# Two-map attention: value products on split operands over pairs of query tiles, with the copies and differences of the turned weights placed behind the exponentials

## What is computed

```python
def diff_attention(q, k, v, pos, slopes, lam):
    # q, k: [B, L, H, 2, d]; v: [B, L, H, 2d];  H = 8, d = 64, L = 1040
    scale = A_HEAD_DIM ** -0.5
    def block(qb, pb):
        s = jnp.einsum('bqhmd,bkhmd->bhmqk', qb, k).astype(jnp.float32) * scale
        ...
        s = s - slopes[None, :, None, None, None] * dist
        p = jax.nn.softmax(s, axis=-1)
        w = p[:, :, 0] - lam * p[:, :, 1]
        return jnp.einsum('bhqk,bkhe->bqhe', w.astype(v.dtype), v)
    return sweep_queries(block, q, pos[None])
```

## Time and profile before

| | us |
|---|---|
| time, median of 3 runs (3290.07 to 3292.62) | 3291.96 |
| time of the profiled execution | 3290.69 |
| its span, first to last instruction | 3288.9 |
| PE busy in it | 3188.6 (97%) |
| DVE busy | 1707.1 (52%) |
| ACT busy | 1131.5 (34%) |
| POOL busy | 997.7 (30%) |
| mean granted TensorE clock | 0.985 |

### The profile page before, as it was taken

The page is one execution under the profiler, slowest core; times in us unless marked ns, Lnnn a source line. Parts: engine busy times, 40 slices in busy tenths (PEclk is TensorE's granted clock), DMA queues, the critical chain, the costliest instruction groups (busy, mean ns, idle before and its releaser), DMA issues.

```text
span 3288.9 us, 52109 instructions
## 1 busy us (share of the span) xinstructions
PE 3188.6 (97%) x20350; PEld 2839.4 (86%) x20350; DVE 1707.1 (52%) x2867; ACT 1131.5 (34%) x2189; POOL 997.7 (30%) x688
## 2 busy tenths in 40 slices
PE   8999999999999999999999999999999999799997
PEld 6677768788888888999899899999999999699997
DVE  5554556765554535666666632277677033522223
ACT  3433333333332214555555541166465111300002
POOL 3112224787773333222222132210000223022222
PEclk9999999999999999999999999999999999799998
DMA  4011112122225112000000012211111341478888
GB/s 160 26 33 33 33 65 103 64 77 78 77 82 207 52 45 98 20 20 20 20 21 26 14 43 79 74 43 48 38 45 50 129 156 51 181 257 315 307 315 291
DMA packets 94214, 312.01 MB, mean 95 GB/s; under 512 B 14690, under 2 KB 27810, under 8 KB 90832
## 3 DMA queue, kind: packets, MB, share of 16 engines
q1 hardware_dynamic: 68448, 248.16, 21.3%
q10 hardware_dynamic: 19424, 42.70, 3.4%
q0 software_dynamic: 6160, 18.63, 2.3%
HBM read 247.91 MB, written 56.22 MB: 92 GB/s over the span
## 4 chain that ended last, share of the span: by engine, by line
PE 54%; DVE 3%; DMA 1%; ACT 1%; issue 1%; POOL 0%; SPq 0%; ACTq 0%; POOLq 0%; DVEq 0%
PE PS L673 14%; PE PS L3162 7%; PE PS L3631 6%; PE PS L661 5%; PE PS L3226 4%; PE PS L3378 4%; PE PS L3193 3%; PE PS L3661 3%; PE PS L3412 3%; PE PS L3454 2%; DVE EB L2837 1%; PE PS L3227 0%; DMA fin<-h_rows 0%; PE PS L3175 0%; DMA h_rows<-y_row_b,pick_s_b 0%
## 5 line engine op out<-in xcount | busy, mean ns | idle before, releaser
L695 POOL CAST w_hi<-ring 128x1024 fp32r<-128x1024 f32 x130 | 138.1, 1062 | 1543.9 <-PE PS L673 401.4
L697 POOL TENSOR_TENSOR w_lo<-ring,w_hi 128x1024 fp32r<-128x1024 f32 x130 | 333.4, 2565 | 10.5
L2247 ACT ACTIVATE EA<-EA,small_sb 128x1040 f32<-128x1040 f32 x144 | 166.6, 1157 | 186.4 <-DVE small_sb L2690 186.3
L2690 DVE CUSTOM_DVE_ANT_0 EA<-PS,biasH,low_a 128x1024 f32<-128x1024 f32 x128 | 163.6, 1278 | 56.3 <-PE PS L3193 56.2
L3162 PE MATMUL PS<-u_hi,w_hi 128*128 128x348 f32 x504 | 173.5, 344 | 0.0
L3162 PE MATMUL PS<-u_lo,w_hi 128*128 128x348 f32 x504 | 162.1, 322 | 0.0
L3162 PE MATMUL PS<-u_hi,w_lo 128*128 128x348 f32 x504 | 161.8, 321 | 0.0
L1643 DVE TENSOR_TENSOR hid_lo<-hid,hid_hi 128x1024 fp32r<-128x1024 f32 x44 | 91.7, 2123 | 118.8 <-ACT hid_hi L1285 118.8
L1735 PE MATMUL PS<-u_hi,w_hi 128*128 128x512 f32 x352 | 146.8, 417 | 3.0 <-POOL w_lo L697 2.3
L1932 PE MATMUL PS<-t_hi,slot_hi 128*128 128x512 f32 x352 | 138.9, 395 | 5.9 <-DVE t_lo L1544 3.3
L3226 PE MATMUL PS<-Va,PTa 128*128 128x128 f32 (+1 forms) x1152 | 139.9, 275 | 0.0
(11 more groups left out here) (502 smaller groups left out, 8639.5 us busy)
## 6 DMA issues: line engine op xcount, KB each, us to landing
ring<-in_stream SPq DMA_DIRECT2D x130, 512.0 KB, 3.5
w_gate_sb<-in_w_gate SPq DMA_DIRECT2D x64, 512.0 KB, 6.8
w_up_sb<-in_w_up SPq DMA_DIRECT2D x64, 512.0 KB, 8.1
w_down_sb<-in_w_down SPq DMA_DIRECT2D x64, 512.0 KB
gu_raw<-in_gate_up SPq DMA_DIRECT2D x22, 1024.0 KB, 5.6
hid_keep<-hid_out SPq DMA_DIRECT2D x17, 512.0 KB, 2.9
hid<-hid_keep ACTq DMA_DIRECT2D x15, 512.0 KB, 16.4
x_keep<-xT ACTq DMA_DIRECT2D x1, 4176.0 KB, 13.8
```

Of the source, the lines that this page charges most:

```text
L695: pool.tensor_copy(w_hi[j][:, :, :], w_raw[j][:, :, :]).then_inc(S["w_rounded"], 1)
L697: pool.tensor_tensor(w_lo[j][:, :, :], w_raw[j][:, :, :], w_hi[j][:, :, :], ALU.subtract).then_inc(S["w_split"], 1)
L2247: act.activation(e[0:m, :], e[0:m, :], ACT.Exp, scale=-1.0, bias=small[0:m, 8 + 2 * par + k:9 + 2 * par + k], accum_out=small[0:m, 12 + 2 ...
L2690: dve.tensor_tensor_reduce(e[0:m, 0:T1], wide(2 * k, T1, m), bias, -1.0, low_a[0:m, t, k:k + 1], ALU.add, ALU.min, low).then_inc(S["aa_max ...
```

## The change

The value products of attention a are made of split parts over groups of tiles, (0,1), (2,3), (4,5) and (6,7,8). The weights' columns of a group (256, or 272 in the last) are now the moving operand and v the stationary one, so the result is turned: features by tokens. ACT copies it (`take_columns`), PE turns it back (`turn_back`), and ACT writes the scaled rows (`results`). The turned weights are copied by ACT in three instructions per tile (`take_pt`, 16 + 512 + 512 columns) and subtracted by DVE in three (`lower_probs`); v gets the same (`lower_values`). PA_hi and PA_lo exist once. The room for them is taken from o_tok: rows of tiles 5 to 8 are staged and stored to a DRAM tensor o_keep by ACT, 64 KB at a time, and read back in four transfers after the last head. The squares are behind the copies now, and the two exponentials have at most a `take_columns` between them.

```diff
+A_GROUPS = ((0, 1), (2, 3), (4, 5), (6, 7, 8))
+HELD = 5
...
 (ACT, head)
-                        if last:
-                            take_pt_meta(h, par, t, False)
                         if after:
                             exp(after[0], (after[1] + after[2]) % 2, after[2], 0)
-                        if before and not last:
-                            square(*before)
-                        if not last:
-                            take_pt_meta(h, par, t, first and t < 2)
+                        if t % 2 == 0 and before:
+                            take_columns(*before)
                         if after:
                             exp(after[0], (after[1] + after[2]) % 2, after[2], 1)
+                        take_pt(h, t)
+                        if t % 2 and before:
+                            squares(*before)
...
 (DVE)
+                def lower_probs(h, t):
+                    m = P if t < NT else META
+                    n, cols = 9 * h + t, probs_slot(t)
+                    dve.wait_ge(S["aa_pt"], 3 * n + 1)
+                    dve.tensor_tensor(PA_lo[0:META, NT, cols], bank(7, m, 3 * P, META), PA_hi[0:META, NT, cols], ALU.subtract).then_inc(S["probs_lo"], 1)
+                    for b in range(2):
+                        tiles = slice(4 * b, 4 * b + 4)
+                        dve.wait_ge(S["aa_pt"], 3 * n + 2 + b)
+                        dve.tensor_tensor(PA_lo[:, tiles, cols], bank(5 + b).rearrange("p (j n) -> p j n", n=P)[:, :, 0:m], PA_hi[:, tiles, cols], ALU.subtract).then_inc(S["probs_lo"], 1)
...
+                def attend(h, par, t, fresh=False, lower=None):
                     scores(h, par, t, 0, fresh)
                     scores(h, par, t, 1, fresh)
                     combine(h, par, t, fresh)
+                    if lower:
+                        lower_probs(*lower)
...
-                            attend(h, (odd + t + 1) % 2, t + 1, first)
+                            attend(h, (odd + t + 1) % 2, t + 1, first, (h, t))
...
 (PE, turn_probs)
+                    for b in range(2):
+                        if n:
+                            pe.wait_ge(S["probs_lo"], 3 * (n - 1) + 2 + b)
...
+                def values(h, g, half):
+                    n, w = 9 * h + A_GROUPS[g][-1], group_width(g)
+                    pe.wait_ge(S["probs_lo"], 3 * n + 2 + half)
+                    if g == 0:
+                        pe.wait_ge(S["values_lo"], 3 * h + 2 + half)
+                    for i in (range(4, NT + 1) if half else range(4)):
+                        v_hi, v_lo = (Va_hi[:, i, :], Va_lo[:, i, :]) if i < NT else (Vam_hi[:, :], Vam_lo[:, :])
+                        for k, (v, probs) in enumerate(((v_hi, PA_hi), (v_hi, PA_lo), (v_lo, PA_hi))):
+                            last = mm(bank(7, w), v, probs[:, i, 0:w], start=(i == 0 and k == 0), stop=(i == NT and k == 2))
...
+                def turn_back(h, g, n):
+                    pe.wait_ge(S["columns_in"], NGA * h + g + 1)
+                    pe.wait_ge(S["probs_lo"], 3 * n + 1)
...
 (PE, head: scores of t+1, then)
+                        if before:
+                            values(*before, 1)
                         kind, c = UNITS[t]
                         unit(h + 1, 1 - odd, kind, c, 0)
                         turn_probs(h, (odd + t) % 2, t, first)
                         unit(h + 1, 1 - odd, kind, c, 1)
-                        if t >= 1:
-                            values(h, odd, t - 1, 18 * h + 2 * t + 1)
+                        if t in (1, 3, 5, NT):
+                            values(h, min(t // 2, NGA - 1), 0)
+                        if before:
+                            turn_back(*before, 9 * h + t)
...
 (POOL, after the last head)
                 for t in range(NT + 1):
+                    if t == HELD:
+                        pool.wait_ge(S["keep_ld"], 32 + 16 * SPILLED)
                     heads_norm(pool, t).then_inc(S["as_np"], 1)
```

More of the change, by code:

```diff
@@ new lines, in take_columns, with home, results @@
+                def take_columns(h, g):
+                    w = group_width(g)
+                    act.wait_ge(S["aa_o"], NGA * h + g + 1)
+                    act.activation(turned_back[:, 0:w], bank(7, w), ACT.Copy).then_inc(S["columns_in"], 1)
+                def home(h, t, m):
+                    return o_tok[0:m, t, bass.ds(h * P, P)] if t < HELD else stage[t - HELD][0:m, :]
+                def results(h, g):
+                    act.wait_ge(S["aa_v"], TURNED_A * h + 4 + g)
+                    if g == NGA - 1 and h + 1 < HEADS:
+                        act.wait_ge(S["values_lo"], 3 * (h + 1) + 1)
+                    for k, t in enumerate(A_GROUPS[g]):
+                        m = P if t < NT else META
+                        if t == HELD:
+                            act.wait_ge(S["keep_st"], KEPT + 16 * SPILLED * h)
+                        seen(act)
+                        act.activation(home(h, t, m), bank(7, P, k * P, m), ACT.Copy, scale=small[0:m, 48 + t:49 + t]).then_inc(S["aa_y"], 1)
@@ L2347, in _ @@
                 sigmoid(0, 0, EARLY_GATES[0], 0)
-                result(HEADS - 1, NT)
-                square(HEADS - 1, NT)
+                results(HEADS - 1, NGA - 1)
+                squares(HEADS - 1, NGA - 1)
                 roots(slice(HEADS - 1, HEADS))
+                act.wait_ge(S["keep_st"], KEPT + 16 * SPILLED * HEADS)
+                for t in range(HELD, NT + 1):
+                    m = P if t < NT else META
+                    act.dma_start(o_tok[0:m, t, :], o_keep[0:m, t - HELD, :]).then_inc(S["keep_ld"], 16)
                 for t in range(NT + 1):
@@ L3229, in head @@
+                def turn_back(h, g, n):
+                    pe.wait_ge(S["columns_in"], NGA * h + g + 1)
+                    pe.wait_ge(S["probs_lo"], 3 * n + 1)
+                    for k, t in enumerate(A_GROUPS[g]):
+                        m = P if t < NT else META
+                        last = turn(bank(7, P, k * P, m), turned_back[:, k * P:k * P + m])
+                    last.then_inc(S["aa_v"], 1)
                 def head(h, odd, first=False):
@@ L3235, in head @@
                             scores(h + 1, 1 - odd, 0)
-                        if t == 0:
-                            pe.wait_ge(S["aa_vf"], 3 * h + 3)
-                            if not first:
-                                pe.wait_ge(S["aa_pt"], 18 * h)
-                            turn(bank(6, P, 0, META), vTa[:, T1:T2]).then_inc(S["aa_v"], 1)
+                        before = None if first and t == 0 or t == NT or t % 2 else group_before(h, t)
+                        if before:
+                            values(*before, 1)
                         kind, c = UNITS[t]
```

260 lines of the change are left out of this document (142 added, 118 removed).

## The result

The changed kernel takes 3452.46 us (median of 4 runs, 3445.59 to 3452.87), the kernel before 3292.29 us (4 runs on the same chip). The ratio is 1.0482, 95% interval 1.0464 to 1.0500: slower by 160 us, where 118 were forecast. That lies inside the wide range (3350 to 3462), near its upper end, outside the forecast's own 3390 to 3435, and on the second rival's 3453.

The account below looks back on a forecast made before the run. PE's list bounds attention a before; afterwards waits between PE and DVE decide. Seven heads 60, last head 19, tail 7 and clock 32 make +118 us: 3410 us, own range 3390 to 3435, wide range 3350 to 3462.

Parts of the forecast that it names:

- the second rival: Clock falls behind nearly every wait, or POOL's 8.6 us stay, or low clock lengthens even steps: about 3453 us, chance 0.20.
- The odd ring: Attention a, odd t: PE's half value product waits for DVE's differences, made behind the next tile's combination; 9.9 us.
- The clock: Half speed behind PE's idle times: 14 in seven heads, five in the last, 19 x 1.7 = 32 us.
- POOL: What POOL's interference costs DVE per head of attention a: bounds 0 and 8.6 us, 4.3 taken.
- t = 0: First step of a head: the turned values wait for both halves of the differences, 9.7 us.
- Even steps: Attention a, even t: PE's list from scores to scores, 8.5 us, is longer than DVE's 8.3.
- The last head: Between reciprocals of tiles 1 and 8: +19 us from the same waits, plus 5 x 1.7 for low clock.
- the tail: After the last head: POOL's four norms and split wait for o_tok's loads; PE +7 us late, bounds +4 and +13.
- The first, that the clock holds: Rival: idle times leave the granted clock alone, so only 60 + 19 + 7 are added: 3378 us, chance 0.20.
- The halves are not waited for: Rival: differences are ready when PE comes to the first half, PE's shorter list makes it faster: 3262 us, chance 0.05.
- Only DVE's own list binds: Rival: DVE's waits for PE are hidden, its list makes 80.2 us a head: 3312 us, chance 0.07.
- PE's list: PE's work per head of attention a: 18.9 us removed, 13.1 and 1.2 added, shrinking by 4.6 us.

Follow-up runs that it names:

- Run 7: Changed kernel, with ACT's copies for odd t and t = 8 between the next exponentials and DVE's differences ahead of the reciprocals; PE's list untouched: 3312.49 us, ratio 1.0064.
- run 3: Changed kernel plus unread filler products in PE's waits ahead of the first halves of the value products, pricing the clock alone: 3405.89 us, ratio 1.0353.
- the last run of experiment 8: Changed kernel with halves, meta scores, copies, differences and tail work reordered, finally turn_back of three groups behind the next scores: 3284.04 us, ratio 0.9976.
- runs 4 and 5: Changed kernel, tail reordered: POOL's split ahead of its norms (3452.76 us); separately, DVE's lower parts of turned tiles 0 to 2 ahead of its norms (3450.51 us).
- run 2: Changed kernel with PE's first halves of value products and the meta scores moved behind the next step's scores: 3350.23 us, ratio 1.0177.
- run 6: Changed kernel with halves and meta scores behind the next scores, plus ACT's take_columns behind the second exponential: 3342.97 us, ratio 1.0159.

## Why the prediction was right, and where it was short

- **The odd ring.** Right. Passes, 1.40 for the exponential (1.53 where `take_columns` stands between), combination, differences, half product and scores follow as written, and PE's wait at t = 1 and 5 was 1.9 us for 2.0. Run 7 changed only the place of the copies and differences, and 140 of the 160 us went with it.
- **The clock: the term that was mis-sized.** The price was about right: 1.7 us each was worked out, t = 1 ran 1.8 and t = 5 1.7 over its ring, and run 3 has 1.5 and 1.6. The count was not. "Of four per head in seven heads I take 14" rested on idle times of 1.8 to 2.7 us. In the changed kernel seven waits were 5.0 us and seven were 3.1 to 3.8, and the clock fell behind all of them; of the fourteen near 1.9 us it fell behind eleven. With the last head's three that is 28 of 31. At t = 8 the fall costs 3.2 us in five heads, since the meta scores and the scores are at half speed too, and 1.5 in the two where the clock rose earlier. Over seven heads t = 1, 3 and 5 ran 31 us over their rings and t = 8, without POOL's part, 19: 50 us, where 24 were in the sum. That is 26 of the missing 42.
- **POOL.** "I take 4.3" between 0 and 8.6. The head shown has 1.6 at t = 2, 1.3 at t = 6, 1.9 at t = 7 and 0.85 at t = 8, 5.7 us, so 10 us more in seven heads. I had not followed the copy at t = 2 on: it also made t = 3's wait long enough for the clock to fall each time.
- **t = 0**, 10.5 for 9.7, makes up 5 us more over seven heads, and most of that is low clock again. Behind filled waits (run 3) it took 9.9 us in five of the heads. In the first head it took 11.6 us, where the clock fell behind a wait of 1.84 us ahead of `turn_values`, and 10.2 in the last run of experiment 8, where it held there. These three come to 41 of the 42 us.
- **Even steps.** Right: t = 4 took 8.6 us for 8.5, with PE idle next to nothing; t = 2 and 6 are this and POOL.
- **The last head**, +26.4 for +27.5, and **the tail**, +6.8 for +7, came out. In the last head four falls took the place of the five in the sum, behind its three halves and one `turn_back`. The tail came out by another path than the one written, runs 4 and 5: the term had POOL's norms and split in it, and DVE's lower parts behind the same loads ended later. That its size agreed was luck.
- **The rivals.** The second, the clock falling behind nearly every wait, had a chance of 0.20 and is what happened. Its 3453 us is close partly by luck, as it priced POOL higher than it was and t = 8 lower. The first, that the clock holds, is out with the same count. "The halves are not waited for" is out with the waits of 1.7 to 5.0 us. "Only DVE's own list binds" gave 80.2 us for a head. Run 7 has 80.1, but there the differences of odd t and t = 8 lie in a wait that the 80.2 count beside them, so the agreement shows nothing.
- **PE's list** was to shrink by 4.6 us a head, and shrank by 3.8. The value products of 256 columns stand 0.118 us apart (thirteen from 1618.43 to 1619.97), as the row of attention b said. The rest is spread over the list, as distances between starts over a head of the last run and of the kernel before show: the old value products took 18.7 us for the 18.9 taken, the new ones 13.3 for 13.1 and the turns back 0.9 for 1.2, while the half units take 0.4 us more than before and scores and meta scores 0.2. The Trainium skill (TensorE: Matmul & The Clock Gate, "Wait — 56ns, not 53.3ns?") has 0.109 there; here, where every product has a weight load of its own, the measured distance is 9% longer. Its rule for the low clock, N/1.2 GHz, gives 0.227 for 272 columns, and there the trace agrees (0.226).

## What to carry to other kernels

When an operand is made of parts, the part that is made last decides, and its place in its engine's list matters more than how long it takes: here the same three differences cost 140 us more behind a combination than ahead of it, in a wait that was there anyway. Price each wait of PE twice, once for itself and once for the half speed behind it, and follow a late start on another engine into the next wait before counting how many of them are long. And when an experiment takes a wait away, look one step on: in run 2 it stood there again, and the engine named by the longest idle time (run 6) was not its cause.

## What the runs showed of the hardware that I had not expected

- In the changed kernel's seven heads the granted clock fell behind 11 of the 14 idle times of 1.7 to 2.2 us ahead of the halves at t = 1 and 5, and held behind three of the same length (1.74, 1.78 and 1.89 us). Windows behind two idle times of 1.89 us, both at t = 5, one with a fall and one without:

```profile
1754.33:1759.33 5.00, 5.00 (x28) 4.83 (x30) 1.19 (x3) 0.00 (x0) 0.00 (x0) 0.66 0.02 3
1853.52:1858.52 5.00, 5.00 (x40) 4.43 (x41) 1.85 (x5) 0.00 (x0) 0.00 (x0) 1.00 0.00 0
```

Behind the seven waits of 1.4 to 1.5 us in run 7 it never fell. In run 7's last head, waits of 2.14 to 2.17 us before `turn_back` were followed by 0.80, 1.00 and 0.60 over 2 us. So the length of an idle time near 2 us does not decide alone; what else does, no run here shows.

- A copy of 16 columns on DVE (0.17 us) took 2.15 us beside POOL's split, and a difference of 348 columns (0.51) took 2.43; they ended 0.03 and 0.4 us behind POOL's instruction. With DVE's list such a stretch moved rather than go away: in run 7 the difference is short, and the copy behind it takes 2.37 us. POOL's own split, 2.39 us long beside the difference, takes 3.71 there, so the one can hold up the other both ways:

```profile
1615.14 2.37 DVE L2736 COPY EA<-meta_a 128x16 f32<-128x16 f32 x1
```

```profile
1613.77 3.71 POOL L707 TENSOR_TENSOR w_lo<-ring,w_hi 128x1024 fp32r<-128x1024 f32 x1
```
